# The second block's five stages as one program block, with operands made inside the previous projection's loop

## The chip, the cores and the metric

The kernel runs on one core of a Trainium2 chip. TensorE (PE) multiplies, VectorE (DVE), ScalarE (ACT) and GpSimd (POOL) do elementwise work, and SyncE (SP) issues the DMAs of weights. Each engine works through its own instructions in order and waits on semaphores for the others. The metric is device time in microseconds, the median of several executions.

## The reference

One forward pass over 512 tokens of width 1024 in fp32: two layers of a first block (projections, attention, an mLSTM, a convolution, an MLP), which the change leaves alone, and then one layer of a second block:

```python
h = rms_norm_2(x, norm1_g[l]); z = h @ w_in[l]
y_a = gmlp_mixer(...)      # gelu, layer norm, causal mix of 128 tokens
y_b = rglru_mixer(...)     # scan; times gelu(gb)
y_c = hgrn2_mixer(...)     # 4 heads of 64; o * rsqrt(mean(o*o per head) + EPS) * g, then times silu(g)
y_d = pool_mixer(...)
mix = jnp.concatenate([y_a, y_b, y_c, y_d], axis=-1)
x = x + mix @ w_out[l]
hf = causal_dwconv(rms_norm_2(x, norm2_g[l]) @ w_up[l], ffn_conv_w[l], ffn_conv_b[l])
gt, val = jnp.split(hf, 2, axis=-1)
x = x + (jax.nn.gelu(gt) * val) @ w_down[l]
gate = jax.nn.sigmoid(rms_norm_2(x, norm3_g[l]) @ w_pg[l])
x = x + (p[l] @ w_pe[l]) * gate
return rms_norm_2(x, final_g)
```

## The kernel before

Activations lie feature-major: a tile is 128 features by 512 tokens, and 1024 features are 8 tiles (k = 0 to 7). Each fp32 product is made of three fast ones: operand and weights are split into a rounded high part and a remainder, the low part. `product` (L448) computes one group, 128 output features, from 8 tiles: for each k weights_high times operand high (L468) and times operand low (L469), then, after a wait for the low part of the weights, weights_low times operand high for all k (L473). That is 24 matmuls of 512 columns.

The weights go through a ring of four slots. SP loads group n when group n-4 is done (L308, `weights_used`). ACT rounds a slot into one of two `weights_high` buffers (`high_part`, L365), and must first see that the group two before is done. POOL subtracts for `weights_low` (`low_part`, L374). An operand tile is split by ACT (high, L713, or with a per-feature gain L723) and DVE (low, L719 or L728). `TokenScale` makes the rms scale of each token: a matmul with ones over `square_sum` (L1215), a first guess on ACT (L1220, L1222) with a table load ahead of each, a refinement on DVE (L1228 to L1233). It is applied only where a product is evicted, so the operand needs x and the gain alone. `SquareSum` adds up x squared on DVE (L1200, L1202).

The second block is five stages, each a `with nc.Block()` of its own, at whose end all engines meet:

- mixer_stage: 18 groups of `in2`, the mixers' work threaded between them by group number. After group 17 come the second half of the gMLP's mix (`mix_values(1)`, L2938 and L2944) and two sums of o squared per head with a matrix of ones in each half (L3023). ACT takes the square root of 128x512 twice (L3132), DVE its reciprocal twice (L2816), and DVE scales and gates (L2817, L2818).
- out2_stage: ACT and DVE split the 8 tiles of `mix`, then 8 groups. DVE adds each to x (L3190) and squares it.
- ffn_stage: ACT and DVE split gain times x (k = 0 to 7), then 44 groups of `up2` in a loop of 4. DVE evicts (L3325), convolves (L3329, L3334), multiplies (L3339) and makes `acted` low (L3341), ACT does the gelu (L3306) and `acted` high (L3308).
- down2_stage: 24 groups (8, 8 and 6 tiles for each of 8 outputs), DVE adds to x (L3237) and squares.
- ple_stage: loads and turns p, splits gain times x, then 16 groups and the final norm.

Of the kernel before, what the change touches and what calls it, by code (L numbers as in the profile page):

```python
# [20 lines left out]
P = 128  # L21
# [426 lines left out]
def product(core, pe, run, i, q, use, f, high, low, kts=KT, width=T, first=True, last=True, m=P, ready=None, cuts=None, between=None, late=0):  # L448
# [11 lines left out]
    cuts = cuts or [(a, b, a) for a, b in parts(width)]  # L460
    w_high, w_low = (w[:, split_slot(run, q), :].rearrange("p (k c) -> p k c", c=P) for w in (core.ring_high, core.ring_low))

    def with_high(k):
        if ready is not None:
            ready(k)
        for a, b, at in cuts:
            to = out[:, at:at + b - a]
            pe.matmul(to, w_high[:, k, 0:m], high(k, a, b), start=(first and k == 0), stop=False, skip_group_check=True)  # L468
            pe.matmul(to, w_high[:, k, 0:m], low(k, a, b), start=False, stop=False, skip_group_check=True)  # L469

    def with_low(k):
        for a, b, at in cuts:
            mm = pe.matmul(out[:, at:at + b - a], w_low[:, k, 0:m], high(k, a, b), start=False, stop=(last and k == kts - 1),  # L473
# [3 lines left out]
    for k in range(kts - late):  # L477
# [4 lines left out]
    for k in range(kts - late):  # L482
        mm = with_low(k)
    for k in range(kts - late, kts):
        with_high(k)
        mm = with_low(k)
    mm.then_inc(core.weights_used.sem, 1)
# [56 lines left out]
def setup_stage(core, a):  # L544
# [40 lines left out]
    with nc.Block() as block:  # L585
        @block.gpsimd
        def _(pool):
            nc.gpsimd.memset(rows, 0.0).then_inc(cleared.sem, 1)
            nc.gpsimd.memset(core.cond, 0.0).then_inc(cleared.sem, 1)
            nc.gpsimd.memset(core.ones, 1.0).then_inc(cleared.sem, 1)  # L590
            nc.gpsimd.memset(core.eps[:, 0:1], LN_EPS).then_inc(cleared.sem, 1)
            nc.gpsimd.memset(core.eps[:, 1:2], RMS_EPS).then_inc(cleared.sem, 1)
            load_vectors(pool, 0, SHARE, pool_loaded)
            first_low_parts(core, pool, core.runs["conv0"])

        @block.sync
        def _(sp):
            sp.dma_start(core.base, a["base"]).then_inc(base_in.sem, 16)
            load_weights(core, sp, SLOTS)
            sp.dma_start(tokens[:, 0:NTX], a["x"][0].rearrange("(n p) c -> p n c", p=P)).then_inc(tokens_in.sem, 16)  # L600
# [3064 lines left out]
```

## Time and profile before

| | |
|---|---|
| median of 3 runs | 3558.85 us (3556.77 to 3561.76) |
| profiled execution, its own time | 3560.26 us |
| its span | 3558.4 us |
| PE busy | 3325.1 us (93%) |
| DVE, ACT, POOL busy | 51%, 33%, 32% |
| mean granted TensorE clock | 0.962 |

The profile gives busy time by engine and by line. The timeline lists instructions in order of time, with the idle time in front of each and what ended it. A table of windows gives the busy time of each engine in each stretch and the granted clock, where 1.00 is 2.4 GHz and 0.50 is 1.2 GHz. The second block lasts from about 2844 us to the end.

### The profile page before, as it was taken

What the parts mean: (1) busy time and instruction counts of PE and PEld (TensorE: products, weight loads), DVE (VectorE), ACT (ScalarE), POOL (GpSimd) and SP (SyncE); (2) the same over time, 40 slices, a digit from 0 to 9 for tenths busy, and PEclk for the clock granted to TensorE, in tenths of its full rate; (3) what the DMA queues carried; (4) which work ended last, traced back from release to release, by engine and by line L of the source; (5) the groups of instructions that cost most, each with busy time, mean ns of one, the idle gap of its engine ahead of it and who ended that gap; (6) DMA issues with size and microseconds to landing.
All of it is one profiled execution on the core that took longest, in us unless ns stands there. A gap on an engine that the chain in (4) does not pass through costs nothing. (4 is left out here: it accounts for less than half of the span.)

```text
span 3558.4 us, 50703 instructions
## 1 busy us (share of the span) xinstructions
PE 3325.1 (93%) x19112; PEld 2693.0 (76%) x19112; DVE 1817.8 (51%) x2675; ACT 1169.2 (33%) x1758; POOL 1122.8 (32%) x555
## 2 busy tenths in 40 slices
PE   6999999899999999996999988998999979799998
PEld 4888577688878888884777666877999757588785
DVE  2969354603358233245786544127433376777525
ACT  2232333522234222124232424224323364333223
POOL 2523001323233232231431013443444333344442
PEclk8999999899999999997999998999999989899998
DMA  6222154022221222221322330332333222233232
GB/s 177 66 58 55 44 160 125 1 65 59 65 59 56 64 65 60 66 60 37 82 72 55 109 101 25 95 99 72 91 90 94 83 65 60 60 95 97 81 94 76
DMA packets 549132, 270.16 MB, mean 76 GB/s; under 512 B 55922, under 2 KB 547146, under 8 KB 548827
## 3 DMA queue, kind: packets, MB, share of 16 engines
q1 hardware_dynamic: 547330, 267.20, 26.5%
q8 instruction: 127, 2.08, 0.2%
q14 instruction: 50, 0.41, 0.0%
q10 hardware_dynamic: 889, 0.30, 0.0%
q0 software_dynamic: 736, 0.17, 0.0%
HBM read 265.50 MB, written 2.10 MB: 75 GB/s over the span
## 5 line engine op out<-in xcount | busy, mean ns | idle before, releaser
L374 POOL TENSOR_TENSOR weights_low<-weight_ring,weights_high 128x1024 fp32r<-128x1024 f32 (+1 forms) x408 | 985.5, 2417 | 1817.8 <-ACT weights_high L365 1776.9
L365 ACT ACTIVATE weights_high<-weight_ring 128x1024 fp32r<-128x1024 f32 (+1 forms) x408 | 409.7, 1006 | 1325.3 <-PE ps L473 1271.6
L468 PE MATMUL ps<-u_high,weights_high 128*128 128x512 f32 (+1 forms) x1440 | 533.9, 380 | 43.5 <-DVE u_low L810 29.5
L469 PE MATMUL ps<-u_low,weights_high 128*128 128x512 f32 (+1 forms) x1440 | 521.8, 373 | 0.0
L468 PEld LDWEIGHTS ps<-u_high,weights_high 128*128 128x128 f32 x1440 | 276.1, 192 | 109.7 <-issue 39.7
L468 PE MATMUL ps<-hidden_high,weights_high 128*128 128x512 f32 x960 | 334.3, 361 | 16.7 <-DVE hidden_low L2386 16.7
L469 PE MATMUL ps<-hidden_low,weights_high 128*128 128x512 f32 x960 | 331.9, 360 | 0.0
L473 PE MATMUL ps<-u_high,weights_low 128*128 128x512 f32 (+1 forms) x1440 | 316.4, 367 | 1.9 <-POOL weights_low L374 1.9
L469 PEld LDWEIGHTS ps<-u_low,weights_high 128*128 128x128 f32 x1440 | 276.2, 192 | 51.5 <-issue 3.4
L1140 DVE SCALAR_TENSOR_TENSOR conv<-conv,vectors 128x512 f32<-128x512 f32 x360 | 293.1, 866 | 31.8 <-DVE conv L1140 28.8
L468 PE MATMUL ps<-mlp_u_high,weights_high 128*128 128x512 f32 (+3 forms) x1024 | 289.4, 312 | 11.1 <-DVE mlp_u_low L2437 7.2
L469 PE MATMUL ps<-mlp_u_low,weights_high 128*128 128x512 f32 (+3 forms) x1024 | 286.9, 311 | 0.0
L473 PEld LDWEIGHTS ps<-u_high,weights_low 128*128 128x128 f32 x1440 | 246.9, 188 | 47.9 <-POOL weights_low L374 2.4
L2422 DVE SCALAR_TENSOR_TENSOR x_features<-ps,modulation,x_features 128x512 f32<-128x512 f32 x120 | 75.7, 659 | 364.9 <-PE ps L473 364.7
L2180 DVE TENSOR_TENSOR arena<-ps,arena 128x768 f32<-128x768 f32 (+3 forms) x48 | 39.6, 825 | 371.5 <-PE ps L473 371.5
L468 PEld LDWEIGHTS ps<-hidden_high,weights_high 128*128 128x128 f32 x960 | 182.4, 190 | 49.3 <-issue 14.8
L468 PE MATMUL ps<-merge_u_high,weights_high 128*128 128x512 f32 x576 | 203.0, 364 | 15.6 <-DVE merge_u_low L810 15.5
L468 PEld LDWEIGHTS ps<-mlp_u_high,weights_high 128*128 128x128 f32 x1024 | 194.1, 190 | 25.9 <-DVE mlp_u_low L2437 7.6
L469 PEld LDWEIGHTS ps<-hidden_low,weights_high 128*128 128x128 f32 x960 | 182.3, 190 | 30.1 <-issue 0.2
L469 PEld LDWEIGHTS ps<-mlp_u_low,weights_high 128*128 128x128 f32 x1024 | 194.1, 190 | 11.5
L473 PE MATMUL ps<-hidden_high,weights_low 128*128 128x512 f32 x960 | 201.8, 356 | 0.0
L469 PE MATMUL ps<-merge_u_low,weights_high 128*128 128x512 f32 x576 | 200.1, 362 | 0.0
(514 smaller groups left out, 5388.2 us busy)
## 6 DMA issues: line engine op xcount, KB each, us to landing
weight_ring<-in_w_in SPq DMA_DIRECT2D x262, 256.0 KB, 3.2
weight_ring<-in_w SPq DMA_DIRECT2D x256, 256.0 KB, 3.1
weight_ring<-in_w_mod SPq DMA_DIRECT2D x192, 256.0 KB, 3.9
weight_ring<-in_w_up SPq DMA_DIRECT2D x88, 256.0 KB, 3.1
weight_ring<-in_w_out SPq DMA_DIRECT2D x48, 256.0 KB, 3.2
weight_ring<-in_w_down SPq DMA_DIRECT2D x32, 256.0 KB, 3.2
weight_ring<-in_w_mla_out SPq DMA_DIRECT2D x32, 128.0 KB, 2.3
weight_ring<-in_w_conv_out SPq DMA_DIRECT2D x32, 128.0 KB, 2.3
```

What stands on the lines that cost most here:

```text
L365: act.activation(core.ring_high[:, split_slot(run, q), 0:n], core.ring[:, slot, 0:n], ACT.Copy).then_inc(core.high_ready.sem, 1)
L374: core.nc.gpsimd.tensor_tensor(core.ring_low[:, split_slot(run, q), 0:n], core.ring[:, (run.first + q) % SLOTS, 0:n], high.bitcast(F32), A ...
L468: pe.matmul(to, w_high[:, k, 0:m], high(k, a, b), start=(first and k == 0), stop=False, skip_group_check=True)
L469: pe.matmul(to, w_high[:, k, 0:m], low(k, a, b), start=False, stop=False, skip_group_check=True)
L473: mm = pe.matmul(out[:, at:at + b - a], w_low[:, k, 0:m], high(k, a, b), start=False, stop=(last and k == kts - 1), skip_group_check=True)
L1140: nc.vector.scalar_tensor_tensor(conv[:, f, a:b], pads[:, f, bass.ds(t + at, b - a)], w_dw[:, bass.ds(t, 1), f], conv[:, f, a:b], ALU.mult ...
L2180: nc.vector.tensor_tensor(dst, gemm(core, 2 + f, w), sig[:, f, 0:w], ALU.mult).then_inc(multiplied.sem, 1)
L2422: ins = nc.vector.scalar_tensor_tensor(x, gemm(core, q % 2)[:, a:b], mod[:, gates + q, j:j + 1], x, ALU.mult, ALU.add)
```

## The change

- One `nc.Block` holds all of the second block. `mixer_stage`, `out2_stage`, `ffn_stage` and `ple_stage` write into it. `down2_stage` is gone, and its groups follow those of `up2` inside `ffn_stage`. The first block keeps a Block for each stage.
- `in2` to `out2`: the mean square of each head is summed for each token as a column of 16 values in each of 128 partitions (`token_squares`, 8 matmuls). It runs, with `mix_values(1)`, between the high and the low half of `in2`'s last group. Square root and reciprocal work on 128x16. `spread_scales` brings the scales back to 128x512 with 16 matmuls against the identity. Tiles of `mix` are split as each is ready, in the order 6, 7, 0 to 5, and `out2`'s first two groups begin with the first six of these.
- `out2` to `up2`: the loop of `out2` also makes `up2`'s operand: ACT gain_high and DVE gain_low of tile k when output k is added. POOL waits for all of `out2` before it clears the pads and makes `up2`'s low parts. The matmul of the token sums goes between the halves of `up2`'s first group.
- `up2` to `down2`: `down2`'s first products wait tile by tile for `acted` low.
- `down2` to `ple2`: as from `out2` to `up2`, with norm3's gain. p is loaded after `out2`, and turned between the halves of `ple2`'s first group.
- `z`, `u3` and the rows of p are placed from the other end of the on-chip memory, so that they can live while the neighbours do.

The core of the diff, indentation left out:

```diff
-def product(..., between=None, late=0):
+def product(..., between=None, late=0, ks=None, done=True):
...
+    if done:
     mm.then_inc(core.weights_used.sem, 1)
```

```diff
 mixer_stage, vector
-evict(17)
 dve.wait_ge(mixed.sem, mixed.at(2))
 nc.vector.tensor_tensor(mix[:, 1], misc, u[:, 1], ALU.mult).then_inc(gmlp_done.sem, 1)
+evict(17)
+dve.wait_ge(std.sem, std.at(1))
+link(nc.vector.reciprocal(token_std, token_std))
...
+for k in (6, 7):
+    split_mix(k)
+for f in range(2):
+    dve.wait_ge(gb_ready.sem, gb_ready.at(f + 1))
+    nc.vector.tensor_tensor(xc[:, f], xc[:, f], gb[:, f], ALU.mult).then_inc(xc_gated.sem, 1)
+    split_mix(f)
+for k in (2, 3):
+    split_mix(k)
...
 for f in range(2):
-    dve.wait_ge(std.sem, std.at(f + 1))
-    link(nc.vector.reciprocal(sq[:, f], sq[:, f]))
-    link(nc.vector.scalar_tensor_tensor(o[:, f], o[:, f], col(core, "c_norm_g"), sq[:, f], ALU.mult, ALU.mult))
-    link(nc.vector.tensor_tensor(mix[:, 4 + f], o[:, f], g_[:, f], ALU.mult))
+    dve.wait_ge(spread.sem, spread.at(f + 1))
+    link(nc.vector.scalar_tensor_tensor(o[:, f], o[:, f], col(core, "c_norm_g"), pairs_bank(f), ALU.mult, ALU.mult))
+    nc.vector.tensor_tensor(mix[:, 4 + f], o[:, f], g_[:, f], ALU.mult).then_inc(normed.sem, 1)
+for k in (4, 5):
+    split_mix(k)
```

```diff
 mixer_stage, tensor
+def token_squares():
...
+    mm = pe.matmul(token_sums[:, x:x + 2], sq[:, f, n * P:(n + 1) * P], core.halves[:, ::HD2], start=True, stop=True)
...
+def spread_scales():
...
+    mm = pe.matmul(pairs_bank(f)[j * HD2:(j + 1) * HD2, n * P:(n + 1) * P], token_std[:, x:x + 1].to_broadcast([P, HD2]),
+                   core.ident, start=True, stop=True, skip_group_check=True)
...
-    product(core, pe, run, i // 4, i % 4, i // 3, i % 3, high, low, width=TX, ready=first_ready if i == 0 else None)
+    product(core, pe, run, i // 4, i % 4, i // 3, i % 3, high, low, width=TX, ready=first_ready if i == 0 else None,
+            between=last_sums if i == 17 else None)
...
-mix_values(1)
-for f in range(2):
-    pe.wait_ge(squared_o.sem, squared_o.at(f + 1))
-    pe.wait_ge(o_copied.sem, o_copied.at(f + 1))
-    pe.matmul(pairs_bank(f), core.halves, sq[:, f], start=True, stop=True).then_inc(sq_summed.sem, 1)
+spread_scales()

 mixer_stage, scalar, after group 17
+gate_conv(0)
+high_part(core, act, run_out, 0, 0)
+act.wait_ge(sq_summed.sem, sq_summed.at(1))
+act.activation(token_std, token_sums, ACT.Sqrt, scale=1.0 / HD2, bias=core.eps[:, 1:2]).then_inc(std.sem, 1)
+act.wait_ge(used.sem, group_done(core, run, 4, 1))
+for f in range(2):
+    round_mix(6 + f, lambda: act.wait_ge(pooled_made.sem, pooled_made.at(f + 1)))
+high_part(core, act, run_out, 0, 1)
+for f in range(2):
+    round_mix(f, lambda: act.wait_ge(gmlp_done.sem, gmlp_done.at(f + 1)))
+gate_conv(1)
+for f in range(2):
+    round_mix(2 + f, lambda: act.wait_ge(xc_gated.sem, xc_gated.at(f + 1)))
+for f in range(2):
+    round_mix(4 + f, lambda: act.wait_ge(normed.sem, normed.at(f + 1)))
```

```diff
 out2_stage, tensor
+for g in range(2):
+    product(core, pe, run, 0, g, 0, g, high, low, width=TX, ready=ready, ks=MIX_ORDER[:6], last=False, done=False)
+for g in range(2):
+    product(core, pe, run, 0, g, 0, g, high, low, width=TX, ready=ready, ks=MIX_ORDER[6:], first=False)
+for g in range(2, KT):
+    product(core, pe, run, g // 4, g % 4, g // 2, g % 2, high, low, width=TX)
 scalar
+for k in range(KT):
+    if k + LEAD < KT:
+        high_part(core, act, run, (k + LEAD) // 4, (k + LEAD) % 4)
+    else:
+        high_part(core, act, core.runs["up2"], 0, k + LEAD - KT)
+    act.wait_ge(free[k % 2].sem, free[k % 2].at(k // 2 + 2))
+    following.gain_high(act, x(k), gain(k), k, TX)
 vector
+for k in range(KT):
+    dve.wait_ge(used.sem, group_done(core, run, k // 4, k % 4))
+    nc.vector.tensor_tensor(x(k), x(k), gemm(core, k % 2, TX), ALU.add).then_inc(free[k % 2].sem, 1)
...
+    squares.add(x(k), k)
+    following.gain_low(dve, x(k), gain(k), k, TX)
```

```diff
 ffn_stage, gpsimd
+pool.wait_ge(used.sem, group_done(core, core.runs["out2"], 1, 3))
 nc.gpsimd.memset(padded[:, :, :, 0:FFN_PAD], 0.0).then_inc(cleared.sem, 1)
-low_parts(core, pool, run)
+low_parts(core, pool, run, run_down)
 tensor
-scale.sum(pe)
 for q in range(4):
-    product(..., ready=(lambda k: split.wait(pe, k)) if q == 0 else None)
+    product(..., ready=(lambda k: split.wait(pe, k - KT)) if q == 0 else None,
+            between=(lambda: scale.sum(pe)) if q == 0 else None)
...
+with pe.Fori(0, 2) as i:
+    for q in range(12):
...
+        product(core, pe, run_down, ..., ready=acted_ready if q < 3 else None)
 scalar
+if last and n == 1:
+    first_high_parts(core, act, run_down)
...
+for g in range(LEAD, run_down.groups + LEAD):
+    if g < run_down.groups:
+        high_part(core, act, run_down, g // 12, g % 12)
+    else:
+        high_part(core, act, core.runs["ple2"], 0, g - run_down.groups)
+    if g % 3 == 1 and g > 3:
+        k = g // 3 - 1
+        act.wait_ge(free[k % 2].sem, free[k % 2].at(pairs + k // 2 + 2))
+        split.gain_high(act, x(k), gain(k), k, TX)
```

## Rows read from the trace of the kernel before

**Rows 1.** Page: busy time, share and instructions by engine.

```profile
PE 3325.1 (93%) x19112; PEld 2693.0 (76%) x19112; DVE 1817.8 (51%) x2675; ACT 1169.2 (33%) x1758; POOL 1122.8 (32%) x555
```

**Rows 2.** Windows: us, busy of PE, PEld, DVE, ACT, POOL, then PEclk, DMA share, GB/s.

```profile
3200.00:3210.00 10.00, 10.00 (x45) 8.19 (x45) 7.41 (x11) 3.28 (x4) 4.62 (x2) 1.00 0.36 104
...
3030.00:3031.00 1.00, 0.00 (x0) 0.00 (x0) 1.00 (x1) 0.00 (x0) 0.00 (x0) 0.66 0.00 0
...
3341.00:3342.00 1.00, 0.00 (x0) 0.00 (x0) 1.00 (x2) 0.00 (x0) 0.00 (x0) 0.50 0.62 186
```

**Rows 3.** Timeline, in2 to out2: start, duration, engine, line, [idle before <-releaser].

```profile
3019.02 2.03 PE L473 MATMUL ps<-u_high,weights_low 128*128 128x512 f32 x8
...
3020.98 1.08 PE L2938 MATMUL ps<-mixers,ones 1*64 1x512 f32 x4
...
3023.01 1.99 PE L3023 MATMUL ps<-mixers,constants 128*128 128x512 f32 x4
...
3024.96 3.35 DVE L2816 RECIPROCAL mixers<-mixers 128x512 f32<-128x512 f32 x1
...
3035.98 8.57 DVE L719 TENSOR_TENSOR mix_parts_low<-mixers,mix_parts_high 128x512 fp32r<-128x512 f32 x8 [1.25 <-ACT mix_parts_high L713]
...
3038.31 0.77 PE L468 MATMUL ps<-mix_parts_high,weights_high 128*128 128x512 f32 x1 [13.32 <-DVE mix_parts_low L719]
```

**Rows 4.** Timeline, out2 to up2: PE's last low half, the sum, the first group.

```profile
3084.91 2.03 PE L473 MATMUL ps<-mix_parts_high,weights_low 128*128 128x512 f32 x8
...
3089.64 1.10 PE L1215 MATMUL ps<-square_sum,ones 128*128 128x512 f32 x2 [2.71 <-PEq L3156]
...
3090.38 9.23 DVE L728 SCALAR_TENSOR_TENSOR u_low<-x_features,vectors,u_high 128x512 fp32r<-128x512 f32 x8 [1.05 <-ACT u_high L723]
...
3100.25 2.00 PE L473 MATMUL ps<-u_high,weights_low 128*128 128x512 f32 x8
```

**Rows 5.** Timeline, up2 to down2.

```profile
3336.46 2.00 PE L473 MATMUL ps<-u_high,weights_low 128*128 128x512 f32 x8
...
3346.62 0.79 PE L468 MATMUL ps<-acted_high,weights_high 128*128 128x512 f32 x1 [8.16 <-ACT weights_high L365]
...
3352.50 0.85 PE L473 MATMUL ps<-acted_high,weights_low 128*128 128x512 f32 x3
```

**Rows 6.** Timeline, down2 to ple2.

```profile
3468.31 1.54 PE L473 MATMUL ps<-acted_high,weights_low 128*128 128x512 f32 x6
...
3489.30 0.39 PE L468 MATMUL ps<-u_high,weights_high 128*128 128x512 f32 x1
```

**Rows 7.** Timeline: one group of out2 on DVE, ACT and POOL.

```profile
3053.50 0.69 DVE L3190 TENSOR_TENSOR x_features<-x_features,ps 128x512 f32 x1 [1.30 <-PE ps L473]
...
3054.31 0.69 DVE L1200 TENSOR_TENSOR mixers<-x_features 128x512 f32 x1
...
3055.04 2.77 DVE L1202 TENSOR_TENSOR square_sum<-square_sum,mixers 128x512 f32<-128x512 f32 x1
...
3053.43 1.06 ACT L365 ACTIVATE weights_high<-weight_ring 128x1024 fp32r<-128x1024 f32 x1 [4.54 <-PE ps L473]
...
3054.57 2.69 POOL L374 TENSOR_TENSOR weights_low<-weight_ring,weights_high 128x1024 fp32r<-128x1024 f32 x1 [2.92 <-ACT weights_high L365]
```

**Rows 8.** Timeline: small matmuls, PE at full clock.

```profile
2977.22 0.66 PE L2882 MATMUL ps<-constants,mixers 128*128 128x128 f32 x4 [2.99 <-ACT x_features L3107]
...
3010.32 0.66 PE L2963 MATMUL ps<-mixers,x_features 128*64 128x128 f32 x8
...
3541.52 1.91 PE L3412 MATMUL ps<-constants,normed 128*128 128x128 f32 x16
```

**Rows 9.** Timeline of DVE: half a round of the up2 loop, its longest instructions.

```profile
3327.51 0.69 DVE L3325 TENSOR_TENSOR ffn_work<-ps,ffn_work 128x512 f32<-128x512 f32 x1 [1.54 <-PE ps L473]
...
3329.03 4.88 DVE L3334 SCALAR_TENSOR_TENSOR ffn_work<-ffn_work,vectors 128x512 f32<-128x512 f32 x4
...
3340.02 2.73 DVE L3334 SCALAR_TENSOR_TENSOR ffn_work<-ffn_work,vectors 128x512 f32<-128x512 f32 x4
```

More of the change, by code:

```diff
@@ L445, in gemm, with product @@
     return bank(core, 2 * f, width)
-def product(core, pe, run, i, q, use, f, high, low, kts=KT, width=T, first=True, last=True, m=P, ready=None, cuts=None, between=None, late=0):
+def product(core, pe, run, i, q, use, f, high, low, kts=KT, width=T, first=True, last=True, m=P, ready=None, cuts=None, between=None, late=0, ks=None, done=True):
     n = split_count(run, i, q)
@@ L472, in with_low @@
         for a, b, at in cuts:
-            mm = pe.matmul(out[:, at:at + b - a], w_low[:, k, 0:m], high(k, a, b), start=False, stop=(last and k == kts - 1),
+            mm = pe.matmul(out[:, at:at + b - a], w_low[:, k, 0:m], high(k, a, b), start=False, stop=(last and k == ks[-1]),
                            skip_group_check=True)
         return mm
-    for k in range(kts - late):
+    for k in early:
         with_high(k)
@@ new lines, in merge_stage, with _ @@
+    block = core.block
+    @block.sync
+    def _(sp):
+        prefetch(core, sp, *(r.name for r in runs))
+    @block.gpsimd
+    def _(pool):
+        low_parts(core, pool, *runs, made=LEAD)
+    @block.tensor
+    def _(pe):
+        high, low = core.u.operands()
+        ready = lambda k: core.u.wait(pe, k)
+        for b, run in enumerate(runs):
+            with pe.Fori(0, 4) as i:
+                for f in range(2):
+                    product(core, pe, run, i, f, 4 * b + i, f, high, low, width=w, ready=ready if b == 0 else None)
+                for f in range(2):
+                    product(core, pe, run, i, 2 + f, 4 * b + i, 2 + f, y_high, y_low, kts=4, width=w,
+                            ready=lambda k: pe.wait_ge(split_made.sem, split_made.at(4 * b + k + 1)))
@@ L3350, in ffn_stage @@
     low_made.passed(n_f + 2)
-    for f in free:
-        f.passed(run.groups // 4)
+    for n, f in enumerate(free):
+        f.passed(pairs + (KT // 2 if n < 2 else 0))
 def ple_stage(core, a, out):
@@ new lines, in _ @@
+        high, low = split.operands()
+        for i in range(rounds):
+            for f in range(2):
+                product(core, pe, run, i, f, i, f, high, low, width=TX, between=sum_and_turn if i == f == 0 else None,
+                        ready=(lambda k: split.wait(pe, k - KT)) if i == f == 0 else None)
+            if i == 0:
+                pe.wait_ge(copied.sem, copied.at(2))
+            for f in range(2):
+                plain_product(core, pe, run, i, 2 + f, i, 2 + f, lambda k, a, b: pt[:, k, a:b], 2, TX)
```

3738 lines of the change are left out of this document (1853 added, 1885 removed).

## The prediction

> **What bounds the kernel now.** I read the page first: PE is busy for 93% of the span and no other engine for more than 51% [rows 1], so time can only be won where PE is idle, runs at the lower clock, or is given less to do. Then the windows. Inside the long loops PE starts 45 matmuls in each 10 us at clock 1.00 [rows 2], one every 0.23 us, and nothing in the change makes those fewer. The gaps of the second block lie at the seams of its stages, so I followed the timeline across each of the four that the change opens. The reader is to see the same picture four times: PE ends a low half, DVE and ACT finish what they have, all engines meet, an operand is made from its first tile, and PE starts at the lower clock. The clock is 0.50 at 3341, 2.5 us after PE stopped, and 0.66 at 3030, 5 us after it stopped [rows 2, 3, 5]. After a pause of 2.7 us at 3087 it is unchanged, since L1215 takes 1.10 us for two matmuls just as later ones do [rows 4].
>
> The pitch of a matmul is (2.03 - 0.40) / 7 = 0.233 us in in2 and out2 and (2.00 - 0.39) / 7 = 0.230 us in up2 [rows 3, 4], taking 0.40 and 0.39 us as what the last of eight lasts. A group of 24 is thus 5.6 and 5.5 us, a low half 1.9 us, a high half 3.7 us.
>
> **The change, seam by seam.** Each is measured from the start of one low half to the start of another, before and after.
>
> Up2 to down2 is the simplest. From 3336.46 to 3352.50 are 16.0 us [rows 5]. The work in it is one low half and one high half, 1.8 + 3.7 = 5.5 us. The rest is DVE's convolution of the last pair, the meeting, and a rounding (ACT, L365) that PE waited 8.16 us for. After the change down2's first rounding runs while up2's last group is multiplied, and its second right at that group's end. The last tile of acted, number 21, is needed only in down2's third group, 11 us after up2's end. DVE made it 6.7 us after that end before. POOL's two subtractions may now hold L3334 up once, by 4.88 - 2.73 = 2.2 us [rows 9], and 8.9 is still under 11. ACT's queue behind the new wait for up2's last group is the gelu of the last pair, which DVE delivers later anyway. Saved: 16.0 - 5.5 = 10.5 us, between 9 and 11.
>
> Down2 to ple2: from 3468.31 to 3489.30, the end of ple2's first group, are 21.0 us [rows 6]. The work in it is six low matmuls (1.4), a whole group (5.5), the sum (0.9) and the turning of p (8 matmuls at 1.91 / 16 = 0.12, so 1.0 [rows 8]): 8.8 us. What stays is the last tile. When down2's last output is done, at T, ACT rounds a weight slot (1.06) and DVE adds (0.69), squares (0.69) and sums (L1202). The last takes 2.77 us where POOL's L374 of 2.69 us started before it and 0.69 where not; it ends as POOL does, plus half a microsecond [rows 7]. Here POOL starts its subtraction as in rows 7, so the sum ends at T + 4.5 and gain_low of tile 7 at T + 5.3. PE can work 3.7 - 0.5 = 3.2 us on tiles 0 to 6, and waits 2.1 us. Saved: 21.0 - 8.8 - 2.1 = 10.1 us, less 0.2 for semaphores: 9.9, between 7.5 (the clock falls) and 12 (POOL holds nothing up). The token scale's chain is next, but its result is wanted only for the eviction, and copies of p by DVE end before ple2's second group does. The tail is as before.
>
> Out2 to up2: from 3084.91 to 3100.25 are 15.3 us [rows 4]. Work: low half 1.9, sum 0.9, high half 3.7, together 6.5. The last tile is later here, because POOL waits for all of out2 and then makes two low parts in a row: T + 0.3 to T + 3.0 and to T + 5.4. I take it that L1200, two reads of on-chip memory like L1202, is held up by the first and L1202 by the second; its own row shows 0.69, since POOL started after it [rows 7]. Then the sum of squares ends near T + 6 and tile 7 near T + 6.9; at the seam before, L728 took 9.23 us for eight with the same two low parts beside it [rows 4]. PE waits 6.9 - 3.2 = 3.7 us. Saved: 15.3 - 6.5 - 3.7 = 5.1. A pause of 3.7 us lies between the 2.7 that left the clock alone and the 5 after which it had fallen, so I charge half of the 3.3 us that a spell of 7 us at half rate costs: 3.5 saved, between 1.5 and 7.5. The Trainium skill, SBUF — State Buffer, section "Who interferes with whom", says that whichever of the two engines issues first holds the shared ports for its whole instruction. By it L1200 waits as well and this seam gives the lower sum, 5.1; without it 7.3. No row shows L1200 starting second.
>
> In the out2 loop DVE's work for each group becomes 0.69 + 0.69 + 2.77 + 0.75 and the steps between, 5.1 us after a start 0.17 after the group's end [rows 7]: just under the 5.6 of PE. Hidden, with 0.3 to spare; without that cover each 0.1 costs 0.7 us in all. ACT's high part for group k+2 stands in front of its wait for DVE's add, never behind.
>
> In2 to out2: from 3019.02, the start of in2's last low half, to 3084.91, that of out2's last, are 65.9 us [rows 3, 4]. After the change, with 3019.0 as the same instant: mix_values(1) 3023.01 - 20.98 = 2.0, token_squares 16 passes of 0.12 [rows 8], 1.9, low half 1.9: 3024.8. ACT's root of 16 columns falls inside it. DVE evicts (0.15 + 0.69) and inverts 16 columns (the 512 take 3.35 [rows 3]; estimate 0.2): 3026.0. spread_scales is 32 passes between (0.66 - 0.1) / 8 = 0.07 and 0.12 [rows 8]; I take 0.09, 2.9 us: 3028.9. Removed are L3023 (2.0) and two reciprocals of 3.35 with the two scalings between them [rows 3]. PE is not waiting for the scales then but for the tiles of mix: ACT can round only once in2 has left the operand (3024.8), does 6 and 7 (1.2), a weight slot (1.06), 0 and 1 (1.2), table load and gelu (1.9), then tiles 2 and 3 with a product by DVE between (1.9): 3032; DVE's share, held up once by POOL for 2.1, ends tile 3 at 3034.5. Tiles 4 and 5 follow at 3038.9, under the products of the first six. So: high half 3035.0, low 1.4, second group's six tiles 4.2, both groups' last two 2.8: 3043.4. Five groups (28.0) and a high half (3.7) later it is 3075.1, against 3084.91: 9.8 saved. PE has four short pauses from 3025 to 3035 and the clock may fall, which I charge with 0.9: 8.9, between 5 and 12.
>
> **The sum.** 8.9 + 3.5 + 10.5 + 9.9 = 32.8 us. The profiled execution took 3560.26, which gives 3527.5; it lies 1.4 above the median, so for the median 3526.0.
>
> **The rivals.** First, *the clock and the shared ports take more*: it falls at both out2 seams and at ple2, and DVE is held up at each. The lower ends, 5 + 1.5 + 10 + 7.5 = 24: 3535. For it stands that three of the four seams leave a pause of 2 us or more; against it that 2.7 left no mark [rows 4]. Second, *everything overlaps*: the upper ends, 12 + 7.5 + 11 + 12 = 42: 3516. It needs POOL's low parts to slip past DVE. Third, *up2 is bound by DVE*. DVE now starts up2's first pair 4 us late, since the token scale is made after the operand. A pair takes PE 11.0 us; DVE's chain idles 1.54 of it [rows 9], so it is 9.4 long, with one hold-up of 2.2 in it. If the shifted phase brings a second one, the chain is 11.6, and 22 pairs lose 0.6 each: 13 us, 3539. The kernel is *slower than before* from a chain of 11.0 + 32.8 / 22 = 12.5 us on, which takes 3.1 us of further hold-ups in every pair: at 13 us, with two more hold-ups a pair beside ACT's later answers, it loses 22 x 2.0 = 44 and ends at 3570. Against it: a chain that lags by 4 us and gains 1.5 a pair has caught up after three pairs, and then POOL and DVE stand as before. Fourth, *the change doesn't do what it says*: the mix tiles, or the last tile of each operand, arrive so late that the seams only move. Then up2 to down2 alone pays, some 12 us, 3546; the old seams' own rows, where first tiles came within 3 us of their start [rows 3, 4], speak against it.
>
> **Chances.** The forecast's case, 28 to 37 us saved, 0.60; the first rival 0.17; the second 0.12; the third 0.05, of which 0.02 ends slower; the fourth 0.04; 0.02 for no change by mixtures of these. What this kernel's measurement can tell from no change is 0.2%, 7 us. Faster by more 0.95, within 0.03, slower 0.02. The range takes in the first two rivals and most of the third: 3514 to 3541.
>
> **What would show it.** Right: no idle PE of over 1 us from up2's last group to down2's; PE idle about 2 us before tile 7 of ple2's operand and 3 to 4 us before that of up2's, each ended by L728's successor on DVE, with a DVE sum of 2.8 us ahead of it; out2's last low half 56 us after in2's, at clock 1.00 most of the way; up2's loop at 5.5 us a group. Wrong: idle PE inside up2's loop ended by DVE's eviction; a matmul pitch other than 0.230 in up2, whose operand now lies at another address; a granted clock of 0.50 over more than 7 us at any seam; out2's groups over 5.6 us apart.

## The result, and the profile after

The changed kernel takes 3530.2 us (median of four, 3528.22 to 3533.69) where the kernel before takes 3560.31 on the same chip (four, 3556.77 to 3568.2): a ratio of 0.9914, 95% interval 0.9901 to 0.9926. That is 30.1 us less. The forecast was 3526.0, 32.8 less, and its range (3514 to 3541) held the time. The profiled execution took 3533.69 us with a span of 3531.9, against 3560.26 and 3558.4.

The page of the changed kernel, busy time by engine (compare [rows 1]). PE's work is the same to 2 us, although 44 matmuls were added; what has gone is idle time.

```profile
PE 3323.5 (94%) x19156; PEld 2689.3 (76%) x19156; DVE 1809.3 (51%) x2674; ACT 1169.7 (33%) x1758; POOL 1121.0 (32%) x555
```

**In2 to out2** (the timeline after, start, duration, engine, line; compare [rows 3]). The low half at 3022.73 takes 3.31 us for 8 matmuls, though PE had not stopped, and out2's first product waits for tiles that DVE makes beside POOL (L2827, one in 2.86 us).

```profile
3020.92 1.95 PE L3005 MATMUL ps<-constants,z 128*128 128x2 f32 x16
3022.73 3.31 PE L475 MATMUL ps<-u_high,weights_low 128*128 128x512 f32 x8
...
3027.07 1.97 PE L3016 MATMUL ps<-constants,small 128*64 128x128 f32 x32 [1.04 <-DVE small L2821]
...
3028.77 2.86 DVE L2827 TENSOR_TENSOR u_low<-mixers,u_high 128x512 fp32r<-128x512 f32 x1
...
3031.69 0.50 PE L470 MATMUL ps<-u_high,weights_high 128*128 128x512 f32 x1 [1.53 <-DVE u_low L2827]
...
3051.04 0.47 PE L470 MATMUL ps<-u_high,weights_high 128*128 128x512 f32 x1 [0.74 <-DVE x_features L3263]
```

The windows of the same profile: PEclk is the last but two of the columns. It is 0.50 in two stretches of the seam, and again at up2's start.

```profile
3021.00:3022.00 1.00, 1.00 (x10) 1.00 (x10) 0.69 (x1) 0.00 (x0) 0.48 (x1) 1.00 0.00 0
3023.80:3024.80 1.00, 1.00 (x4) 0.80 (x3) 0.00 (x0) 0.00 (x0) 0.00 (x0) 0.50 0.00 0
3034.80:3035.80 1.00, 1.00 (x4) 0.71 (x4) 1.00 (x2) 0.34 (x1) 0.00 (x0) 0.50 0.00 0
3088.00:3089.00 1.00, 1.00 (x3) 0.47 (x2) 0.00 (x0) 0.10 (x1) 0.00 (x0) 0.50 0.00 0
```

**Out2 to up2** (timeline after; compare [rows 4]). Two of POOL's subtractions in a row, 5.16 us, and behind each a DVE instruction with two inputs on chip: L1203 (L1200 before) takes 2.45 instead of 0.69, L1205 (L1202 before) 2.71. The last tile follows at 3085.14 and PE has waited 3.39 us.

```profile
3077.24 2.03 PE L475 MATMUL ps<-u_high,weights_low 128*128 128x512 f32 x8
...
3079.51 5.16 POOL L374 TENSOR_TENSOR weights_low<-weight_ring,weights_high 128x1024 fp32r<-128x1024 f32 x2
3080.03 2.45 DVE L1203 TENSOR_TENSOR mixers<-x_features 128x512 f32<-128x512 f32 x1
...
3080.33 0.71 ACT L726 ACTIVATE u_high<-x_features,vectors 128x512 fp32r<-128x512 f32 x1
...
3082.51 2.71 DVE L1205 TENSOR_TENSOR square_sum<-square_sum,mixers 128x512 f32<-128x512 f32 x1
3085.14 0.74 DVE L731 SCALAR_TENSOR_TENSOR u_low<-x_features,vectors,u_high 128x512 fp32r<-128x512 f32 x1
...
3085.94 0.79 PE L470 MATMUL ps<-u_high,weights_high 128*128 128x512 f32 x1 [3.39 <-DVE u_low L731]
...
3087.88 4.11 PE L475 MATMUL ps<-u_high,weights_low 128*128 128x512 f32 x8
```

**Up2 to down2** (compare [rows 5]): one low half after the other, 5.54 us apart, nothing idle.

```profile
3330.77 2.02 PE L475 MATMUL ps<-u_high,weights_low 128*128 128x512 f32 x8
...
3336.31 1.99 PE L475 MATMUL ps<-acted_high,weights_low 128*128 128x512 f32 x8
```

**Down2 to ple2** (compare [rows 6]): the same picture as out2 to up2, with one hold-up.

```profile
3452.12 1.53 PE L475 MATMUL ps<-acted_high,weights_low 128*128 128x512 f32 x6
...
3455.14 2.77 DVE L1205 TENSOR_TENSOR square_sum<-square_sum,ffn_work 128x512 f32<-128x512 f32 x1
...
3458.63 0.50 PE L470 MATMUL ps<-u_high,weights_high 128*128 128x512 f32 x1 [1.70 <-DVE u_low L731]
```

**Up2's loop** (low halves of neighbouring groups, first in the kernel before, then after): they are 5.49 us apart before and 5.60 after. There is no wait in either; eight matmuls take 2.00 and 2.02.

```profile
3199.13 2.00 PE L473 MATMUL ps<-u_high,weights_low 128*128 128x512 f32 x8
...
3204.62 2.00 PE L473 MATMUL ps<-u_high,weights_low 128*128 128x512 f32 x8
```

```profile
3196.37 2.02 PE L475 MATMUL ps<-u_high,weights_low 128*128 128x512 f32 x8
...
3201.97 2.02 PE L475 MATMUL ps<-u_high,weights_low 128*128 128x512 f32 x8
```

Where the 26.5 us of span between the two profiled executions went:

| stretch | before, us | after, us | saved | forecast |
|---|---|---|---|---|
| end of in2's last high half to out2's last low half | 65.9 | 58.4 | 7.5 | 8.9 |
| out2's last low half to the end of up2's first | 17.2 | 14.6 | 2.6 | 3.5 |
| up2's loop | 234.4 | 238.9 | -4.6 | 0 |
| up2's last low half to down2's first | 16.0 | 5.5 | 10.5 | 10.5 |
| down2's loop | 115.8 | 115.8 | 0 | 0 |
| down2's last low half to the start of ple2's second group | 21.0 | 10.7 | 10.3 | 9.9 |
| everything else | | | 0.2 | 0 |

### The profile page after: what moved, and what is told of

Same layout as the page of the kernel before. It is cut to its first block and busy times, and to the rows that moved or that the text cites. A ratio compares the mean times of both kernels' runs of the same rounds, so it can differ in the third digit from the quotient of the medians.

```text
span 3531.9 us, 50658 instructions
## 1 busy us (share of the span) xinstructions
PE 3323.5 (94%) x19156; PEld 2689.3 (76%) x19156; DVE 1809.3 (51%) x2674; ACT 1169.7 (33%) x1758; POOL 1121.0 (32%) x555
## 3 DMA queue, kind: packets, MB, share of 16 engines
q1 hardware_dynamic: 547330, 267.20, 26.7%
## 5 line engine op out<-in xcount | busy, mean ns | idle before, releaser
L470 PE MATMUL ps<-u_high,weights_high 128*128 128x512 f32 (+1 forms) x1504 | 558.5, 380 | 46.3 <-DVE u_low L813 29.9
L471 PE MATMUL ps<-u_low,weights_high 128*128 128x512 f32 (+1 forms) x1504 | 546.3, 373 | 0.0
L470 PEld LDWEIGHTS ps<-u_high,weights_high 128*128 128x128 f32 (+1 forms) x1504 | 286.7, 191 | 116.8 <-issue 38.0
L475 PE MATMUL ps<-u_high,weights_low 128*128 128x512 f32 (+1 forms) x1504 | 338.4, 372 | 1.9 <-POOL weights_low L374 1.9
L471 PEld LDWEIGHTS ps<-u_low,weights_high 128*128 128x128 f32 (+1 forms) x1504 | 286.6, 191 | 55.5 <-issue 3.4
L475 PEld LDWEIGHTS ps<-u_high,weights_low 128*128 128x128 f32 (+1 forms) x1504 | 260.9, 190 | 54.2 <-POOL weights_low L374 2.4
```

## The experiments

The profiles differ by some microseconds ahead of the change's place, of the same kernel too: in2's last group but one starts its low half anywhere from 2997.7 to 3009.7 us. So beside the medians I read one stretch, called S: from that low half to ple2's last. S is 531.8 us before and 506.2 after. Of S too a part is chance, as the sixth experiment shows.

**1. The address of up2's operand.** The changed kernel, with u3 moved back to a multiple of 64 bytes.

```diff
     with ExitStack() as stay:
+        core.space(stay, "spacer", 8, "right")
```

> The changed kernel with a spacer of 8 floats at the right end of the on-chip memory, so that z, u3 and the rows of p lie 32 bytes lower and u3 starts at a multiple of 64 bytes, as it did before the change (now it starts 32 bytes past one). Nothing else differs. Theory A (the address sets the pitch): in up2 a matmul comes every 0.229 us instead of 0.2335, so up2's 42.7 groups between the two seams take 234.4 us instead of 238.9, ple2's products gain another 0.9, and the time falls by 5.5 us against the changed kernel. Theory B (the pitch comes from DVE or POOL standing in another phase, or from the loop's code lying elsewhere): pitch 0.2335 and time unchanged within 1 us.

Measured: 3527.37 us (3525.96 to 3529.53), ratio 0.9906 (0.9892 to 0.9921), S 497.3. The low halves of up2 are 5.49 us apart again.

```profile
3197.78 1.99 PE L475 MATMUL ps<-u_high,weights_low 128*128 128x512 f32 x8
...
3203.28 1.99 PE L475 MATMUL ps<-u_high,weights_low 128*128 128x512 f32 x8
```

S is 8.9 shorter than after. The pitch explains 5.3 (44 groups by 0.105, and 0.7 in ple2). The other 3.6 are the clock, which did not fall at in2 to out2 here (experiment 6). So the loss in up2's loop is the address of the moved operand and nothing else.

**2. All operands at multiples of 64.** The first, with the mixers' arena and the first block's padded too.

```diff
-                core.arena = space(mixer, f"arena{l}", A_CONV)
+                core.arena = space(mixer, f"arena{l}", A_CONV + 8)
...
-            core.arena = core.space(block, "mixers", ARENA2)
+            core.arena = core.space(block, "mixers", ARENA2 + 10)
```

> The run before plus 8 floats at the end of each layer's arena and 10 at the end of the mixers' space, so that every split operand (u, merge_u, branch, hidden, mlp_u, u2, u3) starts at a multiple of 64 bytes instead of 32 past one. Theory A: the pitch of in2 and out2 falls from 0.2335 to 0.229 us as well, and with some 8700 matmuls of the first block's u, hidden, merge_u and branch, and of in2 and out2, at 4.5 ns each the time falls by another 30 to 40 us: 3485 to 3495. mlp_u, whose rows of 772 floats put most tiles off 64 bytes anyway, stays. Theory B: no change.

Measured: 3519.24 (3510.89 to 3526.16), ratio 0.988 (0.9862 to 0.9898), S 496.3. In2's and out2's groups go from 5.60 to 5.44 us, but the first block's hidden layer hardly moves (groups of 24 matmuls from 5.62 to 5.60 us). The expectation of 30 to 40 us was wrong, and with it the rule of 64 bytes: u2 came out at 5.44, u3 at 5.49, the first block nearly nowhere. The median is 8.1 us below the first experiment's and S only 1.0; most of the 8.1 lies ahead of S, and no run tells what of it the padding is and what is chance.

**3. The same padding in the kernel before.**

> The kernel before the change with the same paddings (8 floats after each arena, 10 after the mixers' space); its u3 was at a multiple of 64 bytes already. Theory A: 30 to 40 us less than the kernel before, 3520 to 3530, with up2 as it was. Theory B: as the kernel before.

Measured: 3559.01 (3545.18 to 3565.38), ratio 0.9988 (0.9976 to 1.0), S 531.6. Missed in the same way. Its in2 and out2 groups are at 5.44 as well; 0.16 us by eight groups of out2 is 1.3 in S, and the seams' clock took that back (27.4 instead of 26.7 at in2 to out2, 16.3 instead of 15.3 at out2 to up2). So this padding does not decide between the two kernels: u2 gains the same in both, and only u3 lies differently.

**4. The order of ACT and POOL at two seams.** The changed kernel; out2's and down2's last tiles are rounded ahead of the next weight slot, and POOL makes up2's first two low parts before it waits for out2.

```diff
         for k in range(KT):
+            if k > 1:
+                make(k)
             if k + LEAD < KT:
...
-            act.wait_ge(free[k % 2].sem, free[k % 2].at(k // 2 + 2))
-            following.gain_high(act, x(k), gain(k), k, TX)
...
+        first_low_parts(core, pool, run)
         pool.wait_ge(used.sem, group_done(core, core.runs["out2"], 1, 3))
...
-        low_parts(core, pool, run, run_down)
+        low_parts(core, pool, run, run_down, made=LEAD)
```

> The changed kernel with another order at two seams: in out2 (from the third group on) and down2, ACT makes the gained high part of tile k before it rounds the next weight slot, and POOL makes up2's first two low parts before it waits for all of out2, not after. My theory (tile 7 is late because DVE's sums stand behind POOL's subtraction): POOL starts 1.6 us later after each group, DVE's sum takes 0.69 us instead of 2.77 and gain_low of tile 7 is done 3.1 us after the group, when PE has just finished tiles 0 to 6; the waits of 3.4 us (up2) and 1.7 us (ple2) are gone, the clock stays at 1.00 at up2's first group, and the time falls by 7 to 8 us. Rival (DVE's own four instructions a group are the bound): the waits stay over 1 us and the time falls by under 2 us.

Measured: 3525.59 (3522.95 to 3533.24), ratio 0.9905 (0.9892 to 0.9917), S 498.0, 8.2 less than after. The timeline of the same seam: both sums take 0.69, and POOL starts behind them.

```profile
3078.51 0.69 DVE L1203 TENSOR_TENSOR mixers<-x_features 128x512 f32<-128x512 f32 x1
...
3079.23 0.69 DVE L1205 TENSOR_TENSOR square_sum<-square_sum,mixers 128x512 f32<-128x512 f32 x1
3079.84 0.75 DVE L731 SCALAR_TENSOR_TENSOR u_low<-x_features,vectors,u_high 128x512 fp32r<-128x512 f32 x1
3080.26 2.56 POOL L374 TENSOR_TENSOR weights_low<-weight_ring,weights_high 128x1024 fp32r<-128x1024 f32 x1 [3.01 <-ACT weights_high L365]
```

Out2's last low half to up2's first is 6.06 us instead of 10.64, the next group 6.00 instead of 7.69, down2 to ple2 6.75 instead of 8.72: 8.2 together. The waits for tile 7 are gone from PE's list. Those 8 us were DVE's sums standing behind POOL's subtractions, and the clock that fell in the wait. The edit moved ACT's rounding of tile 7 forward too, but that was not what the tile waited for: in the changed kernel its high part was ready at 3081.0, four microseconds before DVE came to it. The two moves were not run apart.

**5. The wait of up2 to down2 put back.**

```diff
+        pe.wait_ge(low_made.sem, low_made.at(3 + 21))
         with pe.Fori(0, 2) as i:
             for q in range(12):
```

> The changed kernel with one wait more: TensorE waits for all 22 tiles of acted before down2's first group, as the meeting of all engines did before. In the changed kernel down2's first low half starts 5.54 us after up2's last, with no idle PE. Theory A (the forecast's): the overlap of this seam is worth its whole price, 16.0 - 5.5 = 10.5 us. Here the convolution of the last pair stays on DVE and the rounding of the weights is already done, so the low half should come 14 to 16 us after up2's last, some 8 us of idle PE ended by DVE's last u_low or acted_low, with the clock at 0.50 for the first 3 to 4 us after it: the kernel is 9 to 11 us slower than the changed one, near 3540. Rival B: the slack is taken up later, since DVE and the rounding of down2's weights get ahead in the pause: then less than 5 us. The stages after it must not move in either.

Measured: 3545.14 (3543.71 to 3548.09), ratio 0.9951 (0.9936 to 0.9966), S 514.7. Timeline:

```profile
3332.23 2.03 PE L475 MATMUL ps<-u_high,weights_low 128*128 128x512 f32 x8
...
3343.42 0.76 PE L470 MATMUL ps<-acted_high,weights_high 128*128 128x512 f32 x1 [9.16 <-DVE acted_low L3394]
```

Down2's first low half comes at 3349.88, 17.65 us after up2's last, against 5.54: 12.1 more, of which 9.2 is idle and 3 the clock at 0.50 after it. Down2's loop and what follows are as they were. Nothing takes the slack up later (rival B falls); I had set the price 1 to 3 us low. By the ratios to the kernel before (0.9951 against 0.9914) it is 13 us.

**6. A second profile of the changed kernel, unchanged.**

> The changed kernel, unchanged, looked at a second time, for the clock at in2 to out2. In its first profile the clock fell twice there (3.3 to 3.6 us at 0.50 each), in the run on the order it did too, and in three other runs whose code at this place is the same it stayed at 1.00 throughout. If the fall is fixed by the kernel (its tiny matmuls), it is here again and the stretch from in2's last low half to out2's last is 32.1 + 26.3 us as before; if it comes and goes from one execution to the next, either value may show, and any effect of under 3 us at this place is read from runs with the clock at 1.00 only.

Measured: 3527.34 (one execution), S 502.6. The timeline at the place where the clock had fallen:

```profile
3018.18 1.95 PE L3005 MATMUL ps<-constants,z 128*128 128x2 f32 x16
3019.99 2.11 PE L475 MATMUL ps<-u_high,weights_low 128*128 128x512 f32 x8
```

And its windows, PEclk 1.00 (the last but two):

```profile
3023.00:3024.00 1.00, 0.87 (x16) 0.90 (x18) 0.98 (x2) 1.00 (x2) 0.00 (x0) 1.00 0.53 150
3024.00:3025.00 1.00, 1.00 (x21) 0.86 (x16) 1.00 (x3) 1.00 (x3) 0.69 (x1) 1.00 1.10 331
```

The low half takes 2.11, not 3.31. Of the six profiles whose code is the same here (after, 1, 2, 4, 5 and this one), the clock fell in two. From in2's last group but one to out2's last low half these two take 73.1 us; of the four others the three with the same pitch take 70.4 to 70.5. So 2.6 us of this seam are chance, and another 1.0 at out2 to up2 (18.3 or 17.3 for two groups). From here on I compare with S 502.6 where a run's clock stayed up at this seam.

**7. Tiny matmuls and the clock.** The token sums made three times.

```diff
-            for f in range(2):
+            for f in (0, 1, 0, 1, 0, 1):
                 for n in range(4):
```

> The changed kernel with the token sums made three times, 48 passes with 2 moving columns instead of 16 (the same result): 4 us more of tiny matmuls in a row, 5.7 us in all. If tiny matmuls count as rest for the clock, it falls here surely, since 5 us of true rest brought it down at other places: it would be at 0.50 by the low half behind them, which takes 3.3 us or more. If they don't, it stays at 1.00 as in three of the five runs with 16 of them, or falls as by chance. The place itself is longer by 3.5 to 4 us in any case.

Measured: 3543.54 (one execution), S 513.1. The windows: PE is busy with the passes of 2 columns from 3024.0 to 3032.2, and the clock falls on the way.

```profile
3025.00:3026.00 1.00, 1.00 (x12) 1.00 (x11) 0.00 (x0) 0.00 (x0) 0.00 (x0) 1.00 0.00 0
3026.00:3027.00 1.00, 1.00 (x9) 1.00 (x8) 0.00 (x0) 0.00 (x0) 0.00 (x0) 0.65 0.08 16
3028.00:3029.00 1.00, 1.00 (x6) 1.00 (x6) 0.00 (x0) 0.00 (x0) 0.00 (x0) 0.50 0.00 0
3033.00:3034.00 1.00, 1.00 (x4) 0.71 (x4) 0.00 (x0) 0.00 (x0) 0.00 (x0) 0.50 0.00 0
```

The clock is at 0.50 from about 3026.3 to 3036.5, although no idle time lies ahead of or in the 48 passes, and the passes themselves take 8.29 us instead of 3 x 1.95. The fall comes 2.3 us after the first pass, and that is where it came in the two profiles of experiment 6 that had one (2.3 and 2.4 us). So the added passes need not have caused it. What is new is its length, 10 us instead of 3.4: 6 of them are passes, the rest is the low half of 512 columns and a wait of 1.03. Whether tiny matmuls bring the clock down, only keep it down, or neither, one execution does not show; 16 of them left it at 1.00 in four of six profiles.

**8. The group norm on 128 x 512 again**, in the place of the small sums.

```diff
-                    mm = pe.matmul(token_sums[:, x:x + 2], sq[:, f, n * P:(n + 1) * P], core.halves[:, ::HD2], start=True, stop=True)
-            mm.then_inc(sq_summed.sem, 1)
+                pe.matmul(pairs_bank(f), core.halves, sq[:, f], start=True, stop=True).then_inc(sq_summed.sem, 1)
...
-            link(nc.vector.scalar_tensor_tensor(o[:, f], o[:, f], col(core, "c_norm_g"), pairs_bank(f), ALU.mult, ALU.mult))
+            link(nc.vector.reciprocal(sq[:, f], sq[:, f]))
+            link(nc.vector.scalar_tensor_tensor(o[:, f], o[:, f], col(core, "c_norm_g"), sq[:, f], ALU.mult, ALU.mult))
```

> The changed kernel with the group norm of the mixers on 128 x 512 as before (two matmuls with 512 moving columns for the sums, root and reciprocal of 512 columns each), still in the place of the small sums inside in2's last group. Two questions. First the clock: in the changed kernel the low half behind the small sums (16 passes with 2 moving columns, 1.95 us) took 3.31 us for 8 matmuls instead of 1.9, with PE never idle. If the tiny matmuls brought the clock down, the low half here takes 1.9 to 2.1 us, and the start of out2 is not at the lower clock because of them; if it is something else at this seam (the short matmuls of mix_values, the heat of all engines) it stays at 3 us or more. Second what the token-major sums are worth: spread_scales (1.97 us and 1.04 us of waiting) is gone, but two reciprocals of 3.35 us stand on DVE ahead of tiles 4 and 5, which come about 6 us later (3044 instead of 3038), where PE wants them at 3037.5 to 3041.7: 3 to 5 us of waiting. Together 1 to 4 us slower than the changed kernel; 0 or faster would mean that the sums on tokens were worth nothing here.

Measured: 3533.63 (3530.51 to 3536.69), ratio 0.9918 (0.9903 to 0.9933). From in2's last group but one to out2's last low half it takes 75.2 us, against 73.1 after and 70.5 in the second profile; the clock fell twice here as well, a little later (0.50 around 3031 and 3044). The low half behind the sums took 2.42. Tile 4 is late as expected:

```profile
3042.66 0.47 PE L470 MATMUL ps<-u_high,weights_high 128*128 128x512 f32 x1 [3.22 <-DVE u_low L2824]
```

With the falls in both, the token-major sums are worth about 2 us, and 1.4 by the ratios (0.9918 against 0.9914), whose intervals overlap. That part of the change is small beside the 7 to 10 us of this seam; that the rest came from giving PE the tiles one by one is what the timelines suggest, and no run undid it alone.

**9. Another order at in2 to out2.** The token sums after in2's last group, the scales spread behind out2's first two tiles, and tiles 0 to 2 rounded ahead of the second gelu and weight slot.

```diff
-                    between=last_sums if i == 17 else None)
+                    between=(lambda: mix_values(1)) if i == 17 else None)
...
-        spread_scales()
+        pe.wait_ge(o_copied.sem, o_copied.at(2))
+        token_squares()
...
+            if k == MIX_ORDER[2]:
+                core.spread_scales()
```

> The changed kernel with another order at in2 to out2 and nothing else: the token sums come after in2's last group and not inside it, and the scales are spread after out2's first two tiles (6 and 7), so that PE has work while ACT and DVE round the others; ACT rounds tiles 0, 1, 2 ahead of the second gelu and the second weight slot after it; DVE gates the convolution's first half before its last eviction; the root's table is loaded early. If this seam is bound by the order in which ACT and DVE make the eight tiles, as I read it, out2's first two groups end 3 to 5 us sooner than the 25.4 us after in2's last low half that they took, and the kernel is 3 to 5 us faster than the changed one. If tiny matmuls bring the clock down, in2's last low half takes 1.9 to 2.1 us here instead of 3.31, and the clock falls behind the token sums instead, at out2's start. If the clock's fall eats the gain (it falls because PE is thinly used here, whatever the order), less than 1.5 us is won.

Measured: 3528.91 (3524.72 to 3534.11), ratio 0.9907 (0.9892 to 0.9922), S 500.5. Against the second profile that is 2.1 us less; against the first 5.8, of which 3.6 is the clock. Less than the 3 to 5 expected: the waits of 1.0, 1.5 and 0.5 us became one of 1.4, and the spread of the scales still costs PE its 1.97.

**10. The mirror of the first: the kernel before with u3 moved by 32 bytes.**

```diff
+        core.space(block, "spacer", 8)
         core.u = core.features(block, "u3", KT, TX)
+        core.space(block, "spacer2", 8)
```

> The kernel before, with only the operand of up2 and ple2 (u3) moved by 32 bytes, from an address divisible by 64 to one that is 32 past it; the tiles of acted and the work area keep their places to 64 bytes. The mirror of the run in which the changed kernel's u3 was moved back. If the address alone sets the pitch, up2's groups of 24 matmuls go from 5.49 to 5.60 us and ple2's partial and whole groups from 8.94 to 9.03, so from in2's last groups to the end it takes 4.6 + 0.9 = 5 to 6 us more than the 526.3 us of before, and down2 is unmoved. If something else of the changed kernel set the pitch (the engines beside it, the release order), the groups stay at 5.49.

Measured: 3566.49 (3560.44 to 3570.84), ratio 1.0017 (1.0008 to 1.0026), S 537.3, 5.5 more. Up2's groups are 5.60 us apart. But down2's moved too, against the expectation: 5.57, 4.65 and 5.11 us where they were 5.49, 4.58 and 5.04.

```profile
3197.18 2.03 PE L473 MATMUL ps<-u_high,weights_low 128*128 128x512 f32 x8
...
3202.78 2.03 PE L473 MATMUL ps<-u_high,weights_low 128*128 128x512 f32 x8
...
3358.30 2.02 PE L473 MATMUL ps<-acted_high,weights_low 128*128 128x512 f32 x8
3363.87 2.03 PE L473 MATMUL ps<-acted_high,weights_low 128*128 128x512 f32 x8
```

The pitch alone comes to more than 5.5 (down2's loop took 117.6 us instead of 115.8), but the seams around down2 were 1.4 us shorter in this profile. Acted had moved by 64 bytes, from 192 to 0 modulo 256. The rule of 64 bytes fell for good, and a table by the start address modulo 256 took its place, which the last run tested.

**11. All parts together** (1, 2, 4 and 9).

> The changed kernel with all that the runs so far speak for: the operand of up2 and ple2 moved by 32 bytes, the operands of the first block and of the mixers as in the run with all of them moved, the order of ACT and POOL at the two seams as in the run on the order, and the order at in2 to out2 of the run beside this one. If the parts add up: 11 us for the addresses, 5 to 8 for the order, 3 to 5 for the third, from 3530: 3506 to 3512, which would beat both kernels. If the parts share the same gain (the clock), 3514 to 3520.

Measured: 3512.95 (3501.93 to 3519.67), ratio 0.9848 (0.9834 to 0.9863), S 486.7. The parts add up: from 502.6, less 5.3 for u3's address, 1.3 for u2's (eight groups by 0.16), 2.1 for the order at in2 to out2 and 7.2 for the other two seams (8.2, less the 1.0 of chance at up2's start) gives 486.7. The median lies 1 us above the expectation of 3506 to 3512.

**12. The same with u3, acted, u2 and most of the first block at 128 modulo 256.**

```diff
-        core.space(stay, "spacer", 8, "right")
+        core.space(stay, "spacer", 24, "right")
...
+            core.space(inner, "spacer3", 48)
             acted = core.features(inner, "acted", D_FF2 // P, TX)
...
-                core.arena = space(mixer, f"arena{l}", A_CONV + 8)
+                core.arena = space(mixer, f"arena{l}", A_CONV + 24)
```

> The run with all parts together, with nothing changed but the places of operands: u3 (up2, ple2) goes 64 bytes down, acted (down2) 192 bytes up, and the operands of the first block 64 bytes up, so that u3, acted, u2 and the first block's u, hidden and mlp_u all start 128 past a multiple of 256. In the rows so far, start address modulo 256 and time of 24 matmuls with 512 columns: 128: 5.44 (u2, mixers' operand moved); 192: 5.49 (u3 and acted); 0: 5.58 (acted in the run on before with u3 moved: 4.65 and 5.11 where it was 4.58 and 5.04); 96 and 224: 5.60. Theory 64 (only a multiple of 64 bytes matters, as I took it until now): up2 stays at 5.49, down2 at 4.58 and 5.04. Theory 128 (an odd multiple of 64 is good, an even one bad, as acted's fall says): up2 goes to 5.58, down2 to 4.65 and 5.11, 6 us slower in the second block. Theory 256 (the place within 256 bytes): up2 and ple2 go to 5.44 and down2 to 4.54 and 5.0, some 4 us faster over 44 + 18 groups and down2, 3509 from 3513, and the first block's groups move as well, by an unknown amount. Seams as in the run with all parts.

Measured: 3503.73 (3496.35 to 3506.13), ratio 0.9832 (0.9819 to 0.9845), S 482.8, 3.9 less than the run before. Up2 and down2:

```profile
3201.83 1.98 PE L475 MATMUL ps<-u_high,weights_low 128*128 128x512 f32 x8
...
3207.27 1.98 PE L475 MATMUL ps<-u_high,weights_low 128*128 128x512 f32 x8
...
3316.07 1.98 PE L475 MATMUL ps<-acted_high,weights_low 128*128 128x512 f32 x8
3320.61 1.52 PE L475 MATMUL ps<-acted_high,weights_low 128*128 128x512 f32 x6
3325.59 1.98 PE L475 MATMUL ps<-acted_high,weights_low 128*128 128x512 f32 x8
```

5.44 in up2, 4.54 and 4.98 in down2: the table modulo 256 foretold all three, and the two other theories are out. The first block bears it out once more. Its hidden layer's operand went from 32 modulo 256 in the kernel before to 64 in the second experiment and to 128 here, and its groups of 24 matmuls from 5.62 to 5.60 and to 5.44 us (the kernel before, then this one):

```profile
2795.03 2.03 PE L473 MATMUL ps<-hidden_high,weights_low 128*128 128x512 f32 x8
...
2800.65 2.03 PE L473 MATMUL ps<-hidden_high,weights_low 128*128 128x512 f32 x8
```

```profile
2789.13 1.98 PE L475 MATMUL ps<-hidden_high,weights_low 128*128 128x512 f32 x8
...
2794.57 1.98 PE L475 MATMUL ps<-hidden_high,weights_low 128*128 128x512 f32 x8
```

Matmuls overlap, so this shows in their starts; the mean duration of one hardly changes (394 to 391 ns in the low half). This version is the fastest of all, 60 us under the kernel before on its chip. About 49 of that lie in S; the rest is the first block and chance.

## Why the prediction was right, point by point

**The sum** was 32.8 us of seams. The seams gave 30.9 in the first profile (7.5 + 2.6 + 10.5 + 10.3) and 3.6 more in the second, where the clock stayed up longer; the forecast lies between. What it left out is the pitch: 4.6 us lost in up2 and 0.7 in ple2. The median of all runs is 2.7 us less saved than forecast. That the total came so near is in part luck: the seams gave more than forecast where the clock stayed up, and the pitch took it back.

**Up2 to down2**, 10.5 forecast, 10.5 measured. The steps held: the last tile of acted is not waited for, the roundings lie under up2's last group. Putting the wait back costs 12.1.

**Down2 to ple2**, 9.9 forecast, 10.3 measured. PE waits 1.70 us for tile 7 (2.1 forecast), behind a sum of 2.77. The clock stayed up.

**Out2 to up2**, 3.5 forecast, 2.6 and 3.6 measured in the two profiles. The wait is 3.39 (3.7 forecast), and both of DVE's sums were held up, as the step said on the ground of the Trainium skill's page SBUF — State Buffer, section "Who interferes with whom": L1203, for which no row of before showed a second place, took 2.45 behind POOL. Experiment 4 shows the rest of the rule, since both take 0.69 when they start first. The charge for the clock was a guess that happened to fit. It rested on the pause of 2.7 us having left the clock alone, and the trace of before does not bear that out: behind that pause the granted clock was 0.50 from 3091.8 to 3098.6, and at 3341 it was 0.50 only 2.5 us after PE had stopped. In the changed kernel it fell ahead of the last tile's first product or soon after it and was 0.50 for about 7 us in the first profile and 3.4 in the second, behind the same wait (3.39 and 3.38). Half of the 3.3 us was thus the price of the second and too little for the first.

**In2 to out2**, 8.9 forecast, 7.5 measured and 10.0 in the second profile, where out2's last low half starts 55.9 us after the end of in2's last high half. The forecast's 56 counts from there too, although its sign of being right says "after in2's" low half, which now starts 4 us later. Mis-sized were two steps that offset each other: spread_scales takes 1.97 us and not 2.9, and the low half in front and the first products were at the lower clock, 2.6 us where 0.9 was charged. The wait for L2821 (1.04) and the backlog of DVE behind it (0.74 at out2's fourth group, which came 6.57 us after the third and not 5.6, a sign of being wrong that came true once) were not in the sum.

**Up2's loop.** The sum charged nothing. That the operand lies at another address was named as a sign of being wrong, and it came true: 5.60 for 5.49. The step that failed is "nothing in the change makes those fewer" as the whole of the loop's price. The rows of before already held both pitches, 0.233 in in2 and 0.230 in up2, and nobody asked why; at 44 groups the difference was worth 5 us.

**The rivals.** That everything overlaps would have needed POOL to slip past DVE; experiment 4 does it by order and gets those 8 us. Up2 did not become bound by DVE: PE has no wait inside its loop. The tiles did not arrive so late that a seam only moved. The first rival's 24 us took 10 for up2 to down2, whose own lower end was 9; that moves it by 1 us, inside the range.

## What to carry to other kernels

When an engine boundary is taken away, the new end of the seam is the chain behind the last tile; see what the other engines issue right in front of it, for a bulk instruction of POOL or a weight slot of ACT moved by one place was worth 8 us, as much as a whole seam. When buffers move, compare the pitch of the long matmul loops first: here 32 bytes cost 5 us in S, and the best place found gave another 4. And look twice before explaining 3 us at a place where the clock may fall, since the same code gave 70.4 and 73.1.

## What the runs showed of the hardware

**The start address of the moving operand sets the pitch of a matmul.** The time of 24 matmuls with 512 columns, high and low parts alike, at full clock, by the start address that the program gave the operand, modulo 256 bytes:

| modulo 256 | 24 matmuls, us | seen in |
|---|---|---|
| 128 | 5.44 | u2 (experiments 2, 3, 11, 12), u3, acted and the first block's hidden layer (12) |
| 192 | 5.49 | u3 before and in 1, 2, 3, 11; acted everywhere but in 10, 12 |
| 0 | 5.57 | acted in 10 |
| 96 | 5.60 | u2 before and after |
| 224 | 5.60 | u3 after and in 10 |
| 64 | 5.60 | hidden layer in 2, 3, 11 |
| 32 | 5.62 | hidden layer before and after |

The addresses follow from the order and the sizes in which the kernel reserves its buffers; what the runs vary is their difference. Why 128 is the best place and not 0 is open. The weights never moved, so no run tells the operand's own address from its distance to theirs.

**The clock at a seam is partly chance**: it fell in two of six profiles of the same code, which is worth 2.6 us. The Trainium skill, TensorE: Matmul & The Clock Gate, section "What's actually happening", says that the count of slow matmuls varies from run to run for the same kernel. It says so of a kernel's start; the traces agree for the middle of one, where the same eight matmuls took 2.11 or 3.31 us.

**The clock can be down while PE is never idle**: it was 0.50 for 10 us in one execution with 48 passes of 2 columns (experiment 7), 6 of them during the passes. That the passes are the cause is not shown.
